# Attention scores of a decoder layer in two passes over 128 rows instead of three over 64

## The reference

```python
z = jnp.einsum('bhqd,bhkd->bhqk', qb, kb).astype(jnp.float32) * scale      # 8 heads
log_not = jnp.where(strict, jax.nn.log_sigmoid(-z), 0.0)
between = lax.cumsum(log_not, axis=3, reverse=True) - log_not
a = jnp.where(strict, jnp.exp(jax.nn.log_sigmoid(z) + between), 0.0)
...
sc = jnp.einsum('bhqd,bhqmd->bhqm', qblk[g], kg).astype(jnp.float32) * scale   # 3 groups x 4 heads
p = softmax over the window; the groups' outputs are mixed by their denominators
...
x = x + (g_sb * y_sb + g_dl * y_dl) @ w_o[l]
```

## Time and profile before

| | |
|---|---|
| median of 3 runs | 1131.58 us |
| profiled execution | 1133.07 us, span 1131.3 us |
| mean granted TensorE clock | 0.992 |
| PE busy | 1104.0 us (98%), 6039 instructions |
| PEld busy | 943.9 us (83%) |
| DVE busy | 771.8 us (68%) |
| ACT busy | 540.9 us (48%) |
| POOL busy | 0.2 us |
| DMA | 102.99 MB, mean 91 GB/s |

### The profile page before, as it was taken

How to read it: one execution, slowest core, us unless ns; L and a number is a source line. 1 busy time by engine, 2 the same in 40 slices (tenths; PEclk the granted TensorE clock), 3 DMA queues, 4 the chain that set the end, 5 groups by cost and what they waited for, 6 DMA issues and landing times.

```text
span 1131.3 us, 15584 instructions
## 1 busy us (share of the span) xinstructions
PE 1104.0 (98%) x6039; PEld 943.9 (83%) x6039; DVE 771.8 (68%) x1080; ACT 540.9 (48%) x867; POOL 0.2 (0%) x4
## 2 busy tenths in 40 slices
PE   7989999999999999999999999999999999999996
PEld 5878899988998788877777778788898899889985
DVE  6866378745868778678765556667774578637854
ACT  6544156523644456567754443425552255415541
POOL 0000000000000000000000000000000000000000
PEclk9999999999999999999999999999999999999998
DMA  8223233332224212211112112532233223323211
GB/s 288 95 75 106 81 113 112 105 101 93 91 72 133 78 38 75 56 43 59 39 57 72 54 52 95 148 93 93 85 105 109 94 93 112 94 94 112 91 59 74
DMA packets 32905, 102.99 MB, mean 91 GB/s; under 512 B 4161, under 2 KB 5569, under 8 KB 32833
## 3 DMA queue, kind: packets, MB, share of 16 engines
q1 hardware_dynamic: 32832, 102.01, 28.6%
HBM read 99.90 MB, written 2.10 MB: 90 GB/s over the span
## 4 chain that ended last, share of the span: by engine, by line
PE 88%; DVE 6%; ACT 3%; issue 2%; DMA 0%; DVEq 0%; SPq 0%; ACTq 0%
PE acc_pair L1187 25%; PE acc_pair L1189 25%; PE acc_pair L1188 25%; PE pair_bank L1187 2%; PE pair_bank L1189 2%; PE pair_bank L1188 2%; PE bank L1187 1%; PE bank L1189 1%; PE bank L1188 1%; DVE w_lo L767 1%; ACT rope L636 1%; ACT w_hi L479 1%; PE bank L1195 1%; PE bank L1197 1%; PE bank L1433 1%
## 5 line engine op out<-in xcount | busy, mean ns | idle before, releaser
L1187 PE MATMUL acc_pair<-xg_hi,w_hi 128*128 128x512 f32 (+1 forms) x693 | 266.6, 385 | 7.0 <-DVE w_lo L999 7.0
L1188 PE MATMUL acc_pair<-xg_lo,w_hi 128*128 128x512 f32 (+1 forms) x693 | 261.3, 377 | 0.0
L1189 PE MATMUL acc_pair<-xg_hi,w_lo 128*128 128x512 f32 (+1 forms) x693 | 260.2, 376 | 0.0
L479 ACT ACTIVATE w_hi<-w_raw 128x1024 fp32r<-128x1024 f32 (+3 forms) x159 | 154.4, 976 | 149.0 <-PE acc_pair L1189 148.8
L767 DVE TENSOR_TENSOR w_lo<-w_raw,w_hi 128x1024 fp32r<-128x1024 f32 (+3 forms) x159 | 178.7, 1126 | 43.9 <-ACT w_hi L479 39.1
L1187 PEld LDWEIGHTS acc_pair<-xg_hi,w_hi 128*128 128x128 f32 x693 | 131.7, 190 | 29.2 <-issue 7.7
L1189 PEld LDWEIGHTS acc_pair<-xg_hi,w_lo 128*128 128x128 f32 x693 | 131.3, 190 | 24.9
L1188 PEld LDWEIGHTS acc_pair<-xg_lo,w_hi 128*128 128x128 f32 x693 | 131.9, 190 | 20.1 <-issue 0.7
L1189 PE MATMUL acc_pair<-hid_hi,w_lo 128*128 128x512 f32 x352 | 138.8, 394 | 0.0
L1188 PE MATMUL acc_pair<-hid_lo,w_hi 128*128 128x512 f32 x352 | 138.2, 393 | 0.0
L1187 PE MATMUL acc_pair<-hid_hi,w_hi 128*128 128x512 f32 x352 | 136.9, 389 | 0.0
(11 more groups left out here) (217 smaller groups left out, 2060.8 us busy)
## 6 DMA issues: line engine op xcount, KB each, us to landing
w_raw<-in_w13b SPq DMA_DIRECT2D x44, 512.0 KB, 3.6
w_raw<-in_w13a SPq DMA_DIRECT2D x40, 512.0 KB, 3.6
w_raw<-in_wmix SPq DMA_DIRECT2D x22, 512.0 KB, 3.5
w_raw<-in_w2a SPq DMA_DIRECT2D x16, 512.0 KB, 3.6
w_raw<-in_w2b SPq DMA_DIRECT2D x16, 512.0 KB, 3.6
w_raw<-in_wgate SPq DMA_DIRECT2D x8, 512.0 KB, 3.5
w_raw<-in_wend SPq DMA_DIRECT2D x8, 512.0 KB, 3.5
w_raw<-in_wo SPq DMA_DIRECT2D x8, 512.0 KB, 3.5
```

What stands on the lines that cost most here:

```text
L479: act.activation(w_hi[:, s, 0:width], w_raw[:, s, 0:width], ACT.Copy).then_inc(whi_done, 1)
L1187: pe.matmul(o, w_h, r_h, start=first, stop=False, skip_group_check=check)
L1188: pe.matmul(o, w_h, r_l, start=False, stop=False, skip_group_check=check)
L1189: return pe.matmul(o, w_l, r_h, start=False, stop=last, skip_group_check=check)
```

## The change

Five things change.

1. The high and low parts of a head stand in one tile of 128 rows: for queries the 64 rows of the head hold the high part and the other 64 rows the low part (`sq2`, `dq2`), for keys the high part stands in both halves (`sk2`, `dk2`), and the keys' low part stands over 64 rows of zeros (`sk_lo`, `dk_lo`). A score product is then two matmuls over 128 rows: [q_hi; q_lo] by [k_hi; k_hi], and [q_hi; q_lo] by [k_lo; 0].
2. The split of each of the 16 query and key units is two instructions on 64 rows, one for each head, on ScalarE and on VectorE, instead of one on 128 rows.
3. The second copy of the keys' high part is made by two DMAs of 64 rows by 2 KB (128 KB each) per key unit, 12 in all, issued by SyncE behind the weight load of seven units later.
4. GpSimd writes the zeros: two memsets of 64 by 1024 and two of 64 by 512 near the end of the first feed-forward part, two more of 64 by 512 when the last stick-breaking head is done.
5. In MIX_ORDER the keys of a pair come ahead of its queries; the wait on z_done moves with them. Gate unit 6 instead of the last one carries a wait of VectorE for the second `dpv`, since tiles lie elsewhere.

```diff
-MIX_ORDER = ([("q", 0, 0), ("k", 0, 0), ("v", 0, 0), ("q", 1, 0), ("k", 1, 0), ("v", 1, 0),
+MIX_ORDER = ([("k", 0, 0), ("q", 0, 0), ("v", 0, 0), ("k", 1, 0), ("q", 1, 0), ("v", 1, 0),
...
+def split_parts(n):
+    return sum(1 if what in ("v", "rv") else 2 for what, _, _ in MIX_ORDER[:n])
...
+KEYS = [u for u in FINS if mix_kind(u)[0] in ("k", "rk")]
...
+        def stacked(w, head):
+            what, pair, g = mix_kind(w)
+            if what == "q":
+                return sq2[:, pair % 2, head, :]
+            if what == "k":
+                return sk2[:, pair % 2, head, :]
+            return dq2[pair][:, head, g, :] if what == "rq" else dk2[pair][:, head, :]
...
+                if u - 7 in KEYS:
+                    sp.wait_ge(op_hi_done, split_parts(u - 7 - MIX + 1))
+                    for head in (0, 1):
+                        key = stacked(u - 7, head).bitcast(F32)
+                        sp.dma_start(key[head_rows(head + 1), :], key[head_rows(head), :]).then_inc(twin_done, 16)
...
-                    act.activation(dst, src, ACT.Copy).then_inc(op_hi_done, 1)
+                        for head in (0, 1):
+                            rows = head_rows(head)
+                            act.activation(stacked(w, head)[rows, :], src[rows, :], ACT.Copy).then_inc(op_hi_done, 1)
...
+        @block.gpsimd
+        def _(pool):
+            pool.wait_ge(unit_done, chunk_base(FFN_A, len(CHUNKS) - 1) + 2 * CHUNKS[-1][1])
+            for head in (0, 1):
+                pool.memset(sk_lo[head_rows(head + 1), :, head, :].bitcast(F32), 0.0).then_inc(zeros_done, 1)
+            for jp in range(DL_PAIRS):
+                if jp:
+                    pool.wait_ge(pv_done, 2 * SB_PAIRS)
+                for head in (0, 1):
+                    pool.memset(dk_lo[jp][head_rows(head + 1), head, :].bitcast(F32), 0.0).then_inc(zeros_done, 1)
...
-                        dve.wait_ge(op_hi_done, fin)
-                        dve.tensor_tensor(lo[:, pair % 2, :], src, hi[:, pair % 2, :].bitcast(F32),
-                                          ALU.subtract).then_inc(op_lo_done, 1)
+                        dve.wait_ge(op_hi_done, split_parts(fin))
+                        for head in (0, 1):
+                            rows, hi = head_rows(head), stacked(w, head)
+                            lo = hi[head_rows(head + 1), :] if what == "q" else sk_lo[rows, pair % 2, head, :]
+                            dve.tensor_tensor(lo, src[rows, :], hi[rows, :].bitcast(F32),
+                                              ALU.subtract).then_inc(op_lo_done, 1)
...
+                    pe.wait_ge(twin_done, 32 * (KEYS.index(MIX + MIX_ORDER.index(("k", hp, 0))) + 1))
+                    pe.wait_ge(zeros_done, 2)
...
-                            product(o, sk_hi[rows, hp % 2, ks], sk_lo[rows, hp % 2, ks],
-                                    sq_hi[rows, hp % 2, P * i:SEQ], sq_lo[rows, hp % 2, P * i:SEQ],
-                                    n == 0, False, True)
+                            pe.matmul(o, sk2[:, hp % 2, a, ks], sq2[:, hp % 2, a, P * i:SEQ], start=n == 0,
+                                      stop=False, skip_group_check=True)
+                            pe.matmul(o, sk_lo[:, hp % 2, a, ks], sq2[:, hp % 2, a, P * i:SEQ], start=False,
+                                      stop=False, skip_group_check=True)
...
-                    product(bank[0], dq_hi[jp][rows, 0, own], dq_lo[jp][rows, 0, own], dk_hi[jp][rows, :],
-                            dk_lo[jp][rows, :], True, False, True)
...
+                    for g in range(NG):
+                        o = bank[1][:, (g - 1) * P:g * P] if g else bank[0]
+                        keys = own if g else slice(0, SEQ)
+                        pe.matmul(o, dq2[jp][:, a, g, own], dk2[jp][:, a, keys], start=g < 2, stop=False,
+                                  skip_group_check=True)
+                        pe.matmul(o, dq2[jp][:, a, g, own], dk_lo[jp][:, a, keys], start=False, stop=False,
+                                  skip_group_check=True)
```

More of the change, by code:

```diff
@@ L453, in _ @@
             ffn(FFN_A, A["w13a"], A["w2a"], True)
-            for u in range(MIX, GATE):
-                load(u, 0, A["wmix"][u - MIX])
-            for u in range(GATE, END):
-                c, n = GATE_COLS[(u - GATE) % 2]
-                load(u, 0, A["wgate"][(u - GATE) // 2, :, c:c + n])
+            for u in range(MIX, END):
+                if u < GATE:
+                    load(u, 0, A["wmix"][u - MIX])
+                else:
+                    c, n = GATE_COLS[(u - GATE) % 2]
+                    load(u, 0, A["wgate"][(u - GATE) // 2, :, c:c + n])
+                if u - 7 in KEYS:
[3 more added lines that the diff above has]
+                        sp.dma_start(key[head_rows(head + 1), :], key[head_rows(head), :]).then_inc(twin_done, 16)
             for u in range(END, WO):
@@ L653, in _ @@
                         act.wait_ge(raw_done, n + 1)
-                        dst = (sq_hi if what == "q" else sk_hi)[:, pair % 2, :]
                         src = raw[:, w % 2, :]
@@ L657, in _ @@
                         act.wait_ge(rope_step, 2 * (ROPES.index(w) + 1))
-                        dst = dq_hi[pair][:, g, :] if what == "rq" else dk_hi[pair][:]
                         src = roped[:]
@@ L663, in _ @@
                         src = acc[w % RING][:].rearrange("p (b a c) -> p b a c", b=BLK, a=2)
-                    if what == "q" or what == "k":
-                        if pair >= 2 and what == "q":
-                            act.wait_ge(z_done, 3 * (2 * pair - 2))
+                    if what == "k" and pair >= 2:
+                        act.wait_ge(z_done, 3 * (2 * pair - 2))
                     if what == "v" and pair >= 2:
@@ L1054, in _ @@
                         dve.tensor_tensor(roped[:], src, turn, ALU.add).then_inc(rope_step, 1)
-                        hi = dq_hi[pair][:, g, :] if what == "rq" else dk_hi[pair][:]
-                        lo = dq_lo[pair][:, g, :] if what == "rq" else dk_lo[pair][:]
                         dve.wait_ge(rope_step, 2 * t + 2)
-                        dve.wait_ge(op_hi_done, fin)
-                        dve.tensor_tensor(lo, roped[:], hi.bitcast(F32), ALU.subtract).then_inc(op_lo_done, 1)
+                        dve.wait_ge(op_hi_done, split_parts(fin))
+                        for head in (0, 1):
+                            rows, hi = head_rows(head), stacked(w, head)
+                            lo = hi[head_rows(head + 1), :] if what == "rq" else dk_lo[pair][rows, head, :]
+                            dve.tensor_tensor(lo, roped[rows, :], hi[rows, :].bitcast(F32),
+                                              ALU.subtract).then_inc(op_lo_done, 1)
                     else:
                         hi, lo = v_parts(sv[:, pair % 2, :, :] if what == "v" else dv[pair][:])
-                        dve.wait_ge(op_hi_done, fin)
+                        dve.wait_ge(op_hi_done, split_parts(fin))
                         dve.tensor_tensor(lo,
@@ L1362, in _ @@
                     hp, a = w // 2, w % 2
-                    rows = slice(HD * a, HD * a + HD)
-                    pe.wait_ge(op_lo_done, through(("q", hp, 0), ("k", hp, 0)))
+                    pe.wait_ge(op_lo_done, split_parts(through(("q", hp, 0), ("k", hp, 0))))
+                    pe.wait_ge(twin_done, 32 * (KEYS.index(MIX + MIX_ORDER.index(("k", hp, 0))) + 1))
+                    pe.wait_ge(zeros_done, 2)
                     if w == 0:
@@ L1410, in _ @@
                     jp, n = j // 2, DIL * j + r
-                    rows = slice(HD * (j % 2), HD * (j % 2) + HD)
                     own = slice(r * P, (r + 1) * P)
-                    pe.wait_ge(op_lo_done, through(("rq", jp, NG - 1), ("rk", jp, 0)))
+                    pe.wait_ge(op_lo_done, split_parts(through(("rq", jp, NG - 1), ("rk", jp, 0))))
+                    pe.wait_ge(twin_done, 32 * (KEYS.index(MIX + MIX_ORDER.index(("rk", jp, 0))) + 1))
+                    pe.wait_ge(zeros_done, 2 * (jp + 2))
+                    a = j % 2
                     if n:
@@ L1417, in _ @@
                         pe.wait_ge(a_done, 6 * SB_PAIRS)
-                    product(bank[0], dq_hi[jp][rows, 0, own], dq_lo[jp][rows, 0, own], dk_hi[jp][rows, :],
-                            dk_lo[jp][rows, :], True, False, True)
-                    for g in (1, 2):
-                        product(bank[1][:, (g - 1) * P:g * P], dq_hi[jp][rows, g, own], dq_lo[jp][rows, g, own],
-                                dk_hi[jp][rows, own], dk_lo[jp][rows, own], g == 1, False, True)
+                    for g in range(NG):
[5 more added lines that the diff above has]
+                                  skip_group_check=True)
                     pe.matmul(bank[0], identb[:], mask_g0[:, r, :], start=False, stop=True, skip_group_check=True)
```

42 lines of the change are left out of this document (22 added, 20 removed).

## The result

The changed kernel takes **1134.95 us** (median of 20 runs, 1132.04 to 1138.58), the kernel before 1131.51 us (20 runs, 1128.27 to 1135.61). The ratio is 1.0033, 95% interval 1.0023 to 1.0044: slower, by 3.4 us. The forecast was 1127.1 us in a range to 1133, so both the sign and the range were missed. The profiled execution of after took 1134.41 us.

The account below looks back on a forecast made before the run. TensorE was taken as the bound before 456 and after about 574 us, VectorE and ScalarE between. 2.4 us lost by turn 4 less 6.9 saved after gave -4.5, so 1127.1 us from the 1131.58 median; range 1121 to 1133.

Parts of the forecast that it names:

- TensorE's two blocks: On TensorE, a head's scores go from 2.94 to 1.62 us, a block of dilated scores from 1.94 to 1.25.
- rival B: Switching cost stays with bf16: blocks save only 0.45 us, heads 0.64, total 1130.5 us; chance 0.23.
- Ten late blocks, 6.9 us: After turn 4, ten blocks of dilated scores each save 0.69 us, with no split there: 6.9 us.
- Head 0, net 0: Head 0's scores wait about 1.3 us for VectorE instead of 0.70, offset by the 1.32 saved in them.
- The splits: 16 query and key units each gain an instruction on VectorE (0.60 us) and ScalarE (0.52), costing the path 0.5 to 1.1.
- At head 4 2.0 us ahead: At head 3's end 2.0 us are saved; the path leaving TensorE at head 4's scores is 3.0 ahead.
- 456 to 571 us, +7.4: Splits on the path of VectorE and ScalarE add 3.8 us from 456 to 517 us and 3.6 from 517 to 571.
- Turn 4, +2.4: TensorE reaches turn 4 2.4 us late, at 575.9 us, just behind block 4's scaling, and is the bound again.
- Rival C, the clock: New waits at heads 0, 5, 6, 7 and turns 0 to 3 drop TensorE's clock: up to 12 us, 1139; chance 0.09.
- Rival D: Copies for head 0 land 2 us after its split, with a longer clock drop: +2, 1129.1 us; chance 0.10.
- the copies at nothing: Key copies cost nothing, later ones having 5 us and more before their scores; head 0's were charged 0.3 us.
- Rival A: Path not bound by the vector engines, TensorE keeps its savings: about 1111 us, half of it 1119; chance 0.12 for either.

Follow-up runs that it names:

- no_double: Changed kernel with single 128-row splits of each query and key on ScalarE and VectorE (scores not the reference's): 1121.19 us, ratio to before 0.9908.
- fine_waits: Changed kernel with VectorE's low part of the first head waiting for ScalarE's first instruction alone: 1131.86 us, ratio to before 1.0000.
- qk_single: Changed kernel with single splits for the 8 stick-breaking queries and keys alone, rope units still doubled (scores not the reference's): 1132.60 us, ratio to before 1.0012.
- order_only: Kernel before with keys projected ahead of queries in the stick-breaking pairs and the wait on z_done moved: 1131.77 us, ratio 0.9999.
- last_pair_only: Kernel before with two passes for the second dilated pair alone, 4 of 16 units split in two, with finer waits: 1127.91 us, ratio 0.9986.
- pool_half: Changed kernel with the second head's high and low part of each query and key unit made by GpSimd: 1130.30 us, ratio to before 0.9991.
- pool_lo: Changed kernel with GpSimd making the second head's low part alone, ScalarE both high parts: 1132.66 us, ratio to before 1.0011.
- splits_only: Kernel before, still three passes, with each query and key split doubled on ScalarE and VectorE and nothing else: 1147.37 us, ratio 1.0139.
- dve_double: Changed kernel with ScalarE's splits single and VectorE's still doubled (scores not the reference's): 1128.41 us, ratio to before 0.9978.

## Why the prediction was wrong, by its own steps

- **TensorE's two blocks: right.** 1.57 and 1.19 us against 1.62 and 1.25. The full-height mask stands 0.12 us behind its forerunner (402.74 behind a 128-column product at 402.62) and rival B, switching that stays, falls.
- **Ten late blocks, 6.9 us: right**, 7.45.
- **Head 0, net 0: +0.2 us** at its running sums in this pair of traces, though the wait grew by 2.1 and not 0.6 (2.84 against 0.70). That is luck of the pair, as the item on the medians below shows.
- **The splits: the step that failed.** The list had 9.0 us for them up to turn 4, 2.0 of it covered there, so 7 us; they cost 13.5, net of all that was covered (after less no_double), and 12.2 in the kernel with three passes. Three sizes were off. First, the rope units: 0.5 to 1.1 us each in the list, 6.1 for the last seven of the eight; 1.27 each measured, 10.2 for the eight. The 0.52 between two starts on ScalarE was no price for a second half (0.76 here), and the choice, unit by unit, whether one engine's half or both lie on the path leaned too often to one; fine_waits shows that VectorE's longer wait alone was 3 us. Second, k 1, q 1, k 2 and q 2 had little or no price, as lying beside a TensorE that is last; qk_single gives the six units 3.4 us. Up to head 4 the doubled splits cost 2.7 us, where I had 1.7, all at head 3. Third, the cover at turn 4: the prediction let TensorE's slack of 2.0 us swallow a part. Measured, the cost grew with every turn, 9.7 us at turn 0, then 10.9, 12.0 and 13.5 at turn 3 (after less no_double), because ScalarE's prob is what TensorE waits for at turns 1 to 3 (3.40, 2.45 and 1.89 us), and from there to turn 15 nothing is given back.
- **At head 4 2.0 us ahead: 1.6** by the table (72.92 less 71.31). That looks right and isn't: without the doubled splits it is 4.35. The 3.0 us lead on the path that leaves there wasn't reached: counted from head 0, ScalarE's first instruction for head 4 starts 0.8 us earlier than before (455.09 less 396.71 against 455.67 less 396.50) and 3.5 earlier in no_double (452.45 less 396.82), so the doubled splits took 2.7 us of it.
- **456 to 571 us, +7.4: +10.1** between head 4 and turn 4. **Turn 4, +2.4: +8.5.** The sum with these sizes is 8.5 less 7.45, +1.1 us inside the stage.
- **From 1.1 us in the stage to 3.4 us in the medians.** The two profiled executions differ by 1.3 us. The rest is not in this pair; where it stands, other traces suggest. The first running sum of head 0 starts at 396.50, 393.25 and 394.46 us in the three traces with a wait of 0.7 us ahead of the scores of head 0 (before, order_only, last_pair_only), on the mean 394.7, and at 397.2 on the mean of the twelve traces with two-pass scores, where that wait is 2.4 to 4.4 us. The 2.4 us between them and the 1.1 make 3.5. That is an estimate from single executions of kernels that differ, so it is argued and not shown. It fits the clocks: the median of the mean granted clock is 0.988 in the 20 runs of after and 0.995 in the 93 runs of before that stand beside the experiments. The profiled execution of before, at 0.992, is slower than 14 of its 20 runs, and that of after, also at 0.992, is one of the three with the highest clock of its 20.
- **Rival C, the clock: there, and small in this trace.** One drop that isn't hidden, at 520 to 524 us, clock 0.68, and 0.89 in the 4 us after it: 4 x 0.32 + 4 x 0.11 = 1.7 us at most. Behind the waits of 3.40, 2.45 and 1.89 us at the turns it stayed at 1.00. By the item above the clock behind the wait of head 0 may be worth some 2 us more in the medians.
- **Rival D and the copies at nothing: in part wrong.** At head 0 the copies cost 0.3 us in after, what the prediction had charged, but they would hold the scores back even with single splits (no_double). At head 6 TensorE waits 2.0 us for one, of which moving the copies gives back 0.2 to 1 us. The 5 us that I saw ahead of the later scores were no margin: a copy lands 4.3 us after its issue, and the last key's was issued 1.3 us after its split, behind a load.
- **Rival A** falls for the changed kernel. Half of it would have been 1119 us, and only without the doubled splits does the kernel come near (no_double, 1121 us).
- **The signs.** The two blocks, turn 4 to the end and TensorE's busy time (20.2 us less) came as named. The waits for spA_lo at heads 5, 6 and 7, of 2, 5 and 2 us, did not: there is one, of 1.7 us at head 6, and the rest of the time goes at the products with the values (5.4 of the 6.8 us, and the 3.2, in the list of waits) and at the scores of head 6.

That the doubled splits cause the loss is shown, by adding them alone and by taking them away alone. So is which units carry it. What stands ahead of head 0 in the medians is an estimate.

## What to carry to other kernels

Halving an instruction's rows didn't shorten it on VectorE or ScalarE (0.68 and 0.63 us on 64 rows as on 128), so a layout that TensorE likes is paid for by the engines that write it: price each added instruction at its full length, on both engines, in a row, wherever they share one chain. Before splitting one, see whether a transfer can move the half (two steps here took 2.2 to 2.4 us each), and let the consumer of the first half wait for that half alone. A profile names one cause of a wait; another that ends at nearly the same time shows only when the first is taken away, as the copies did at head 0. A kernel whose chain is 88% TensorE can still be bound by the other two for 120 us, and these are the places where an added instruction counts.

## What the runs showed of the hardware

- GpSimd's subtraction of 64x512 takes 1286 ns beside VectorE's (pool_half) and 1293 without it (pool_lo); VectorE's takes 686 ns alone, 1273 on the mean beside GpSimd's, and up to 1.83 us. GpSimd's cast takes 609 ns with VectorE waiting and 1308 beside it.
- The step from products of 64 rows to products of 128 and back costs 0.09 to 0.11 us each time. A change in the second number of the profile's shapes costs nothing that shows: in after the products with the values alternate between 128*128 and 128*64, and start 0.24, 0.17 and 0.18 us apart (404.11, 404.35, 404.52, 404.70), as products of one shape do behind 512 and 384 columns (0.23 and 0.18).
- TensorE's clock behind the same wait isn't the same from run to run. Before and last_pair_only are alike up to the scores of head 0 and wait 0.70 us there; behind it the granted clock of 384 to 388 and 388 to 392 us was 0.78 and 0.80 in the one, and 1.00 and 1.00 in the other. With longer waits it was 0.61 and 0.96 in after (2.84 us), 0.51 and 0.50 in splits_only (2.54), and 1.00 and 1.00 in dve_double (2.65). The first rows of before, last_pair_only and dve_double:

```profile
384.00:388.00 4.00, 4.00 (x19) 2.82 (x18) 1.36 (x3) 3.25 (x7) 0.00 (x0) 0.78 0.30 119
```
```profile
384.00:388.00 4.00, 4.00 (x20) 2.93 (x19) 1.79 (x4) 3.66 (x8) 0.00 (x0) 1.00 0.28 116
```
```profile
384.00:388.00 4.00, 4.00 (x23) 3.27 (x24) 1.33 (x4) 3.03 (x7) 0.00 (x0) 1.00 0.26 102
```

  Between before and last_pair_only the start of head 0's running sums moves by 2.0 us (396.50 and 394.46), of which 0.4 stand ahead of the scores already (383.29 and 382.86). Between dve_double and splits_only, a stretch at full clock and one that is mostly at 1.2 GHz, it is 5.8 us (394.31 and 400.14), more than the whole effect of the change, though these two kernels differ in their scores as well. So single traces were compared from head 0 on, and medians decided.
- A transfer of 128 KB within SBUF lands 2.2 to 2.5 us (medians) after its issue from GpSimd's queue, 2.3 us from SyncE's when the load ahead of it was issued 3 us or more earlier, and 4.3 us when a 512 KB load was issued 0.4 us ahead of it.
